# Linear attention, first block: four places for raw weights, and ScalarE's rounding placed ahead of its x work and of the output's squares

## The reference

```python
h = rmsnorm(x, g) * (1 + scale) + shift
q, k, v, g_lr, r = split(h @ w_in)                   # 512, 512, 1024, 16, 1024 columns
log_a = log_sigmoid(g_lr @ w_alpha + b_alpha) / 16
o = causal attention in chunks of 64, with decay a, over 4 heads
o = rmsnorm(o, norm_g) * silu(r)
x = x + gate * (o @ w_out)
out = rmsnorm(x, final_g)                            # the input of the second block
```

## Time and profile before

| | us |
|---|---|
| median of 3 runs | 2650.35 (2646.22 to 2656.89) |
| the profiled execution | 2648.54 |
| its span, first to last instruction | 2646.5 |
| TensorE busy in it | 2470.5 (93%) |
| VectorE, ScalarE, POOL busy | 1687.6, 1008.9, 694.6 |

### The profile page before, as it was taken

One profiled execution on the slowest core, in us unless ns is written; L12 is line 12 of the kernel. 1 busy time (PEld: TensorE's weight loads), 2 busy tenths in 40 slices (PEclk: granted clock), 3 DMA queues, 4 the chain that ended last, 5 costly groups with the idle time before them and its releaser, 6 DMA issues. The chain is left out here.

```text
span 2646.5 us, 33253 instructions
## 1 busy us (share of the span) xinstructions
PE 2470.5 (93%) x11265; PEld 1698.2 (64%) x11265; DVE 1687.6 (64%) x2746; ACT 1008.9 (38%) x1766; POOL 694.6 (26%) x313
## 2 busy tenths in 40 slices
PE   3898899999999998999999976999999999988997
PEld 1576677777777777777777763554555445546776
DVE  3236564654656461889997984777777777775664
ACT  4144444444345440332222123555445445451222
POOL 1233211111211100102000003677666566640000
PEclk8999999999999999999999996999999999998999
DMA  7964787388668747488767654111111110104334
GB/s 269 358 201 141 245 289 279 132 278 318 210 220 282 275 150 271 174 283 318 236 224 240 213 177 104 49 49 54 31 31 29 30 30 25 27 25 169 131 136 153
DMA packets 225145, 453.62 MB, mean 171 GB/s; under 512 B 23957, under 2 KB 82571, under 8 KB 224756
## 3 DMA queue, kind: packets, MB, share of 16 engines
q1 hardware_dynamic: 193960, 351.04, 39.3%
q10 hardware_dynamic: 31052, 100.87, 11.1%
HBM read 328.86 MB, written 109.35 MB: 166 GB/s over the span
## 5 line engine op out<-in xcount | busy, mean ns | idle before, releaser
L2121 DVE TENSOR_REDUCE att_mx<-att_bank_m 128x1 f32<-128x512 f32 (+1 forms) x640 | 365.2, 629 | 128.9 <-PE att_bank_m L1930 128.9
L2070 ACT ACTIVATE att_p_f<-att_bank_s 128x512 f32<-128x512 f32 x576 | 312.4, 599 | 284.1 <-PE att_bank_s L1971 276.0
L1915 POOL TENSOR_TENSOR att_den<-att_den,att_p_f 128x1024 f32<-128x1024 f32 x160 | 379.4, 2371 | 42.7 <-ACT att_p_f L2070 27.4
L1618 DVE SCALAR_TENSOR_TENSOR proj_conv_acc<-proj_conv_in,proj_conv_w,proj_conv_acc 128x512 f32<-128x512 f32 (+1 forms) x480 | 337.4, 772 | 0.0
L562 PE MATMUL gla_bank_g<-mid_a_hi,mid_w_hi 128*128 128x512 f32 x768 | 310.8, 405 | 2.0 <-POOL mid_w_lo L515 1.1
L562 PE MATMUL gla_bank_g<-mid_a_hi,mid_w_lo 128*128 128x512 f32 x768 | 300.8, 392 | 0.0
L562 PE MATMUL gla_bank_g<-mid_a_lo,mid_w_hi 128*128 128x512 f32 x768 | 300.1, 391 | 0.0
L1945 PE MATMUL att_bank_o<-att_p_f,att_v 128*64 128x512 f32 x1152 | 270.6, 605 | 0.0
L562 PEld LDWEIGHTS gla_bank_g<-mid_a_hi,mid_w_hi 128*128 128x128 f32 x768 | 144.9, 189 | 48.3 <-issue 18.5
L1945 PEld LDWEIGHTS att_bank_o<-att_p_f,att_v 128*64 128x64 f32 x1152 | 74.6, 137 | 146.0 <-issue 104.9
L562 PEld LDWEIGHTS gla_bank_g<-mid_a_hi,mid_w_lo 128*128 128x128 f32 x768 | 144.6, 188 | 31.5
(11 more groups left out here) (404 smaller groups left out, 4753.7 us busy)
## 6 DMA issues: line engine op xcount, KB each, us to landing
mid_w_hi<-scratch_w_hi SPq DMA_DIRECT2D x100, 512.0 KB, 4.5
mid_w_lo<-scratch_w_lo SPq DMA_DIRECT2D x100, 512.0 KB, 6.1
mid_w_hi<-scratch_w_hi ACTq DMA_DIRECT2D x84, 512.0 KB, 3.9
mid_w_lo<-scratch_w_lo ACTq DMA_DIRECT2D x84, 512.0 KB, 5.0
scratch_w_hi<-mid_w_hi SPq DMA_DIRECT2D x54, 512.0 KB, 6.3
scratch_w_lo<-mid_w_lo SPq DMA_DIRECT2D x54, 512.0 KB, 7.1
mod_wslab<-in_ada_w SPq DMA_DIRECT2D x6, 2048.0 KB, 18.4
first_w_raw<-in_gla_w_in SPq DMA_DIRECT2D x24, 512.0 KB, 6.7
```

Source lines behind the costliest of these rows:

```text
L1618: dve.scalar_tensor_tensor(acc, src, conv_w[:, c, k:k + 1], acc, ALU.mult, ALU.add).then_inc(taps, 1)
L1915: pool.tensor_tensor(den[s][:], pair(0) if j == 1 else den[s][:], pair(j), ALU.add).then_inc(den_pool, 1)
L2070: act.activation(p_f[:, kt, :], S[kt % SBANKS][:], ACT.Exp, scale=float(HD) ** -0.5).then_inc(p_done, 1)
L2121: dve.reduce_max(mx[:, qt, n:n + 1], M[p % MBANKS][:, 0:min(TB, KEYS - TB * n)], AX_X).then_inc(mx_read, 1)
```

## The change

Three parts, all in block 0:

1. Raw weights have four places in place of two (`raw_at`): the two that were there and two more, in the memory that `w_hi[3]` and `w_lo[3]` take from block 1 on. Tiles 2 and 3 are loaded when the block's program begins, and then tile n+4 is loaded after tile n's halves are stored, where it was n+2. The counts of the landing semaphores follow, and ScalarE waits for all 32 subtractions before it writes the first later tile over a raw place.
2. In unit t, ScalarE rounds tile 17+2t ahead of the squares and not behind them.
3. In the output projection the rounding of tile 25 stands in turn c = 0 with that of tile 26 behind it, and each of the others, up to tile 31, stands behind the square of x1 and ahead of the turn's work on the next block's x.

```diff
+        raw_at = (*w_raw, *keep["w_raw_here"])
+        RAWS = len(raw_at)
...
-        w_landed = keep["w_landed"]
+        w_landed = keep["w_landed"] + [sem(f"w_landed{i}") for i in range(2, RAWS)]
...
+        def raw(n):
+
+            return raw_at[n % RAWS][:]
...
-                    if n >= 2:
-                        sp.wait_ge(w_rest, UP + n - 1)
-                    sp.dma_start(w_raw[n % 2][:], src[:, :, at + col0:at + col0 + P]).then_inc(w_landed[n % 2], 16)
+                    if n >= RAWS:
+                        sp.wait_ge(w_rest, UP + n - RAWS + 1)
+                    sp.dma_start(raw(n), src[:, :, at + col0:at + col0 + P]).then_inc(w_landed[n % RAWS], 16)
...
-                        sp.wait_ge(w_rest, UP + NW - 1 + m)
+                        sp.wait_ge(w_rest, UP + NW - 3 + m)
...
+                for n in range(2, RAWS):
+                    load_raw(n)
                 for b in range(NB):
                     for j in range(NW):
                         if b == 0:
                             keep_split(j)
-                        load(b * NW + j + 2)
+                            if j + RAWS < NW:
+                                load_raw(j + RAWS)
+                        if b * NW + j + 2 >= NW:
+                            load(b * NW + j + 2)
...
-                        act.wait_ge(w_landed[n % 2], UP + 16 * (n // 2) + 16)
+                        act.wait_ge(w_landed[n % RAWS], UP + 16 * (n // RAWS) + 16)
...
-                        act.activation(w_hi[n % 3][:], w_raw[n % 2][:], ACT.Copy).then_inc(w_rounded, 1)
+                        act.activation(w_hi[n % 3][:], raw(n), ACT.Copy).then_inc(w_rounded, 1)
                     m = later_tile((n - 1) // NW, (n - 1) % NW)
                     if m is not None:
-                        act.wait_ge(w_landed[m % 2], UP + 16 * (NW // 2) + 16 * (m // 2) + 16)
+                        if m == 0:
+                            act.wait_ge(w_rest, UP + NW)
+                        act.wait_ge(w_landed[m % 2], UP + 16 * (NW // RAWS) + 16 * (m // 2) + 16)
...
                         act.wait_ge(ot, UP + u * 2)
+                        if b == 0:
+                            round_next(4 + t // 2, 2 * (t % 2))
                         for h in range(GLA_H):
...
-                        round_next(b * 8 + 4 + t // 2, 2 * (t % 2))
+                        if b:
+                            round_next(b * 8 + 4 + t // 2, 2 * (t % 2))
...
                     for c in range(KT):
-                        round_next(b * 8 + 6 + c // 4, c % 4)
+                        if b or c == 0:
+                            round_next(b * 8 + 6 + c // 4, c % 4)
                         if c and b + 1 < NB:
                             square_x1(c - 1)
+                        if b == 0 and c + 1 < KT:
+                            round_next(6 + (c + 1) // 4, (c + 1) % 4)
                         if c in (2, 3) and b + 1 < NB:
                             squares_of_x(b + 1, c - 2)
...
+        w_hi, w_lo = ([sb(f"w_{part}{s}", [P, KT, P], F32R) for s in range(3)] for part in ("hi", "lo"))
+        with ExitStack() as same_places:
+            w_raw_here = [same_places.enter_context(nc.sbuf_tensor(f"mid_w_raw{s}", [P, KT, P], F32)) for s in (2, 3)]
+        w_hi.append(sb("w_hi3", [P, KT, P], F32R))
+        w_lo.append(sb("w_lo3", [P, KT, P], F32R))
```

More of the change, by code:

```diff
@@ L514, in ahead @@
                         pool.wait_ge(w_rounded, UP + n + 2)
-                        pool.tensor_tensor(w_lo[(n + 1) % 3][:], w_raw[(n + 1) % 2][:], w_hi[(n + 1) % 3][:].bitcast(F32),
+                        pool.tensor_tensor(w_lo[(n + 1) % 3][:], raw(n + 1), w_hi[(n + 1) % 3][:].bitcast(F32),
                                            ALU.subtract).then_inc(w_rest, 1)
@@ L2502, in mixing_and_projections @@
         sb, _, sem = pools(nc, ctx, "mid")
-        keep = dict(keep, a_hi=sb("a_hi", [P, KT, TB], F32R), a_lo=sb("a_lo", [P, KT, TB], F32R), x1=sb("x1", [P, KT, TB]),
-                    w_hi=[sb(f"w_hi{s}", [P, KT, P], F32R) for s in range(4)],
-                    w_lo=[sb(f"w_lo{s}", [P, KT, P], F32R) for s in range(4)],
+        w_hi, w_lo = ([sb(f"w_{part}{s}", [P, KT, P], F32R) for s in range(3)] for part in ("hi", "lo"))
[3 more added lines that the diff above has]
+        w_lo.append(sb("w_lo3", [P, KT, P], F32R))
+        keep = dict(keep, w_raw_here=w_raw_here, w_hi=w_hi, w_lo=w_lo, a_hi=sb("a_hi", [P, KT, TB], F32R), a_lo=sb("a_lo", [P, KT, TB], F32R), x1=sb("x1", [P, KT, TB]),
                     u_early=[sem(f"u_early{h}") for h in range(2)], pair_early=[sem(f"pair_early{s}") for s in range(4)])
```

## The result

| | before | after |
|---|---|---|
| median, us (6 runs each, same chip) | 2652.55 (2646.22 to 2656.89) | 2635.20 (2633.90 to 2641.07) |
| the profiled execution | 2648.54 | 2634.41 |
| its span | 2646.5 | 2632.4 |

The ratio is 0.9943, with a 95% interval of 0.9931 to 0.9956: 0.57% faster, and a second series of the same kernel gave 0.9941 (0.9927 to 0.9954). The forecast was 2635 as a median. It was counted from a median before of 2650.35, and the six runs here gave 2652.55, so in the medians the gain is 17.4 us, in the profiled executions 14.1, where -15.0 was forecast: that the median after comes within 0.2 us of the forecast is in part luck.

A forecast was written before the change was run, and what follows sets the result against it. TensorE is busy 2470.5 of 2646.5 us, so only its idle time and half clock in the first block count. Units -8.0, output stage -8.0, early stage +1.0 sum to -15.0: 2633.5 profiled, about 2635 as median; range 2627 to 2647.

The forecast's parts named there:

- Units, -8.0: First block's four attention units: earlier rounding keeps POOL's subtraction off VectorE's root chain; 6.5 us plus 1.5, between 0 and 10.0.
- The lock on s_mid: Rival, attention units: the moved subtraction blocks VectorE's L1060 instead, 2.4 us a unit plus 1.6 of clock; 2659 us, chance 0.06.
- Output stage, -8.0: First block's output stage: POOL-ended waits go; 12.4 us towards the later block's 51.10, less 1.6 and 2.8.
- Tile 24's half clock: Output stage: the wait for gating stays, so tile 24 still runs partly at half clock; 1.6 us given back.
- The clash of tile 31's subtraction with the addition: End of output stage: tile 31's subtraction lands over the start of VectorE's chain to a_lo; 2.3 us given back.
- Early stage, +1.0: Before the units: deeper raw loading delays the slabs of w_mod_2; 1.0 us lost, between 0 and 4.6.
- the landing by turns: Early stage: the last slab lands as before, as a fuller SP queue has little more to take; by volume up to 3.0 us later.
- round-robin rule: Early stage: DMA engines alternate over queue rows, so a longer SP backlog costs a slab nothing; sum 1.0 us lower.
- Keeping binds the output stage: Rival, output stage: roundings wait for late stores of tile n-3, ahead of the x work; stage gains 4, 2639 us, chance 0.17.
- No effect: Rival: roundings stand earlier in the program but wait for matmuls or stores and start as before; about 2650 us, chance 0.06.
- The twin is reached: Rival: first block becomes as short as the later block, clock holds, no clash; -22.4 + 1, 2629 us, chance 0.15.
- It starts at 2637, 0.6 of the forecast: Chance of "faster" (about 0.5%, from 2637 us): 0.6 of the forecast, all of twin, a little of keeping; 0.52.

The follow-up runs named there:

- 1 and 2: Experiment 1 is units alone, experiment 2 is POOL held back, each against the kernel before; medians 2643.26 and 2642.25 us.
- experiment 6: Edits to the changed kernel: tile 31 rounded earlier, 2632.54 us; tile 24 rounded earlier, 2635.16; raw tiles 2 and 3 loaded earlier, 2634.32; all three together, 2626.02.
- three further edits: The changed kernel with tiles 31 and 24 rounded earlier and raw tiles 2 and 3 loaded ahead of the block; 2626.02 us, ratio 0.9899 to the kernel before.
- units and order: The changed kernel with two raw places in place of four, both moves of ScalarE's order kept; median 2640.89 us, ratio 0.9964 to the kernel before.
- units alone: The kernel before with only tile 17+2t's rounding moved ahead of the squares in the first block's units; median 2643.26 us, ratio 0.9961.
- POOL held back: The kernel before, no rounding moved; POOL waits with tile 17+2t's subtraction until the unit's inverse root is done; median 2642.25 us, ratio 0.9962.
- order alone: The kernel before with only the output stage's new rounding order, two raw places; median 2650.75 us, ratio 0.9988.
- the last two kernels of the table: The changed kernel with all three edits, 2626.02 us; and the same with tile 28 rounded after the two squares of x, 2627.30 us.
- places and order: The changed kernel without the move in the units: four raw places and the output stage's new order; median 2644.14 us, ratio 0.9972 to the kernel before.
- places alone: The kernel before with only four raw places, loaded four tiles ahead, ScalarE's order as before; median 2648.07 us, ratio 0.9988.

## Why the prediction was right

*Units, -8.0: measured -7.8.* Each of three intervals went from 22.0 to 19.9, and the fourth unit from 17.43 to 16.01, 1.4 for the 1.5 taken. The cause is shown by two kernels that remove the same overlap in different ways (1 and 2). ScalarE's wait for the root is 2.63, the 2.6 that was named.

*The lock on s_mid: absent.* L1079 took 0.86 to 0.87 for two under the subtraction. The Trainium skill (SBUF — State Buffer, "Who interferes with whom") had this side right: one tile from SBUF and one from a bank went undisturbed, while L1127, with two SBUF inputs, was held until the subtraction was over.

*Output stage, -8.0: measured -6.1.* The stage lasted 57.35 where 55.5 was forecast. The starting point, the twin's 51.10, and both deductions were of the right kind and too small. Tile 24's half clock was priced at 1.6, by tile 27 (tile 24's own length in the kernel before, 7.25, gives the same); it cost 8.45 - 5.68 = 2.8. The clash of tile 31's subtraction with the addition happened as worked out (the starts were 0.14 apart), but was priced at 2.3, the delay alone; with the half clock that follows TensorE's wait it cost 8.09 - 5.08 = 3.0, as experiment 6 shows. The 0.5 for small clashes was 0.6. The terms that were too small are thus the two in which the clock stands: tile 24's was taken over from another tile's, and the clash was given none. For the same reason the stage has two half-clock stretches (at 281.5 and 336.1 us), where one was named. Nor is -6.1 a property of the two output parts alone: without the units' move they gave -8.0, and the units' move without them gave -2.6 there.

*Early stage, +1.0: measured 0.0.* The length is that of the landing by turns, but the way to it is not. Slab 2, the one that the prediction read, took 13.1 us in place of 11.0, and its wait went from 1.98 to 4.04, more than the 1.5 that the prediction allowed. The wait for slab 3 then all but went, the one for slab 5 went and a new one of 4.01 for slab 4 came; in all the waits are 1.5 shorter, and a further 3.4 us at half clock take that back. So the 0.0 is a cancellation that the prediction did not have, and luck in it; the kernel with four places alone has the same one (135.5). The Trainium skill's round-robin rule (DMA: Bandwidth & Descriptors, "Queues, rings and completion order"), read as in the prediction, has the sum 1.0 lower, and the length agrees; that a longer SP backlog costs a slab nothing, which the prediction drew from it, is not what slabs 0 to 2 show. The two misses, 1.9 and 1.0, partly cancel: -13.9 for -15.0.

*Keeping binds the output stage: not in the change* (POOL ended no wait of TensorE there, and no store one of ScalarE's), but it appears when tile 24 is earlier (3.36 us of ScalarE and 1.9 of TensorE, 6), where I had priced it at 4. *No effect: out.* *The twin is reached:* not by the change; by the change with three further edits, to 1.5 us.

*"It starts at 2637, 0.6 of the forecast":* the measured ratio is 0.57% below 1, just beyond the bound of 0.5%, and its interval (0.44% to 0.69%) straddles the bound. A chance near one half fits that; one result cannot test it.

*Left open:* why the stretch to unit 0 is 132.9 in one kernel and 135.4 to 135.7 in four others with the same loads in it (units and order against before, units alone, POOL held back and order alone), and 129.8 against 133.0 in the last two kernels of the table. In the one of 132.9 the waits for slabs came out shorter, 6.2 us in three against 9.6 before. The three edits together gained more than the sum of their single gains: in the block's profile 9.4 against 3.0 + 2.9 + 1.3; of that, 2.4 lie in the stretch to unit 0, so part may be this same scatter. An order in which tile 28 meets neither the store nor the squares was not tried.

## What to carry to other kernels

When GpSimd works on SBUF, ask which VectorE instruction is queued behind it on the critical chain, however small: a 128x4 operation took 2.31 us in place of 0.16 here, and moving the subtraction by a few us inside a unit, without making anything faster, gave over half of the gain. Two measures that each do next to nothing (more buffers; an earlier slot in a queue: 1.0 and 0.3 us here) can be worth most of the stall together (8.0), when the work needs both its input and its turn: test them in pairs. And price each wait of TensorE with the clock behind it: after the one of 3.9 us here the tile took 2.8 longer than at full clock, and the one of 2.5, which was 2.1 longer than in experiment 6, cost 3.0. Last, when a stage keeps its length, look whether its waits and its clock have kept theirs.

## What was not expected of the hardware

A wait of nearly the same length ahead of the same tile was followed by three different things: 3.5 us, then full clock (tile 24 in 5.68, places and order); 3.5 us, then half clock for part of it (7.25, before); 3.9 us, then half clock for most of it (8.45 at 0.64, the change). The first came in two kernels (places alone, too), the second in two (order alone, too), the third in every kernel with a wait of 3.9. So the wait alone does not tell what the clock does next. With 1.7 us of waiting (6) the tile ran at full clock.

A stretch at half clock also stood at 148.4 with no wait right before it:

```profile
148.18 0.44 PE L573 MATMUL gla_bank_g<-mid_a_lo,mid_w_hi 128*128 128x512 f32 x1
148.42 0.63 PE L573 MATMUL gla_bank_g<-mid_a_hi,mid_w_lo 128*128 128x512 f32 x1
```

What came ahead of it is L691, eight matmuls over 32 rows in 3.6 us; but these stand there before the change too, where no stretch follows. It is in every kernel that had a half-clock stretch at 115 to 119 us, and in none in which that one came at 125 us or later, or not at all; with units and order, where the earlier one lasted 3.4 us and not 6.8, it came at 144.2. What ties the two together was not tested.

The subtraction's effect on gating grows with the overlap: three of L1071 took 1.81 undisturbed, 3.27 with the subtraction over part of them (before), and 4.00 here, where it started with the first.
